# Half of the memory weight strips through one transfer and two engines, and the memory input prepared earlier

## The reference

```python
def first_block(x, mem, ...):
    hn = rmsnorm(h, norm_mix_g[l])
    proj = hn @ w_in[l]
    fq, fk, fv, ff, gq, gf, gi, gg = jnp.split(proj, split_idx, axis=-1)
    fox_out = fox_attention(to_heads(fq), to_heads(fk), to_heads(fv), log_f)   # 8 heads of 64
    rec = hgrn2_chunkwise(gq, gf, gi, lbs[l])                                  # 4 heads of 128
    rec = rmsnorm(rec, hgrn_norm_g[l]) * jax.nn.silu(gg)
    h = h + jnp.concatenate([fox_out, rec], axis=-1) @ w_out[l]
    mem_n = rmsnorm(mem, norm_mem_g[l])                                        # 256 x 1024
    h = h + memory_cross_attention(rmsnorm(h, norm_x_g[l]), mem_n, w_xq[l], w_xkv[l], w_xo[l])
    ...
# in memory_cross_attention: kv = mem_n @ w_kv (1024 x 2048), split into k and v
```

## Time and profile before

| | us |
|---|---|
| median of the three runs | 2054.51 |
| the three runs | 2054.51, 2051.1, 2054.57 |
| the profiled execution | 2046.84 |
| its span (first to last instruction) | 2044.7 |

### The profile page before, as it was taken

One profiled execution on the slowest core, in us unless ns is written; L12 is line 12 of the kernel. 1 busy time (PEld: TensorE's weight loads), 2 busy tenths in 40 slices (PEclk: granted clock), 3 DMA queues, 4 the chain that ended last, 5 costly groups with the idle time before them and its releaser, 6 DMA issues.

```text
span 2044.7 us, 26571 instructions
## 1 busy us (share of the span) xinstructions
PE 1924.6 (94%) x9426; PEld 1587.1 (78%) x9426; DVE 990.2 (48%) x1614; ACT 1101.0 (54%) x1526; POOL 272.1 (13%) x318
## 2 busy tenths in 40 slices
PE   5989978899899999999999999989999989999996
PEld 4777767787688888878878778878877868888885
DVE  4176643243442231446886777567661354223134
ACT  6545565452533333355478788668665454334342
POOL 1100001110111111111111111111111101111110
PEclk9999988899899999989999999999999999999998
DMA  8854548873789998978977667876869858898884
GB/s 240 177 114 104 124 112 195 176 166 83 164 192 194 192 193 192 195 158 186 198 155 175 153 145 170 214 183 145 225 144 216 189 121 198 191 196 192 193 179 105
DMA packets 96360, 349.94 MB, mean 171 GB/s; under 512 B 10712, under 2 KB 10712, under 8 KB 95744
## 3 DMA queue, kind: packets, MB, share of 16 engines
q0 software_dynamic: 45216, 163.60, 44.1%
q1 hardware_dynamic: 46512, 169.14, 29.9%
q10 hardware_dynamic: 4528, 15.81, 2.2%
HBM read 344.24 MB, written 4.28 MB: 170 GB/s over the span
## 4 chain that ended last, share of the span: by engine, by line
PE 73%; DVE 10%; ACT 6%; DMA 5%; issue 3%; DVEq 2%; ACTq 1%; SPq 0%
PE bank L350 19%; PE bank L352 19%; PE bank L351 19%; DVE ssum L1848 4%; DMA wl<-in_weights 3%; DMA arena<-scratch 2%; PE bank L459 2%; PE bank L460 1%; PE bank L461 1%; ACT wl L867 1%; PE work L428 1%; ACT wh L866 1%; DVE xt L1881 1%; PE bank L365 1%; PE bank L367 1%
## 5 line engine op out<-in xcount | busy, mean ns | idle before, releaser
L866 ACT ACTIVATE wh<-raw 128x1024 fp32r<-128x1024 f32 x314 | 331.9, 1057 | 649.6 <-PE bank L352 556.1
L350 PE MATMUL bank<-XAh,wh 128*128 128x512 f32 x1400 | 554.4, 396 | 24.5 <-DMA wl<-in_weights 22.6
L352 PE MATMUL bank<-XAh,wl 128*128 128x512 f32 x1400 | 547.1, 391 | 0.0
L351 PE MATMUL bank<-XAl,wh 128*128 128x512 f32 x1400 | 546.9, 391 | 0.0
L848 POOL DMA_DIRECT2D wl<-in_weights x314 | 271.9, 866 | 1739.6 <-ACT wl L867 1700.5
L350 PEld LDWEIGHTS bank<-XAh,wh 128*128 128x128 f32 x1400 | 264.4, 189 | 82.6 <-DMA wl<-in_weights 23.2
L867 ACT ACTIVATE wl<-raw 128x1024 fp32r<-128x1024 f32 x314 | 327.5, 1043 | 0.0
L352 PEld LDWEIGHTS bank<-XAh,wl 128*128 128x128 f32 x1400 | 264.0, 189 | 56.4
L351 PEld LDWEIGHTS bank<-XAl,wh 128*128 128x128 f32 x1400 | 264.7, 189 | 54.2 <-issue 0.7
L350 PE MATMUL bank<-XBh,wh 128*128 128x512 f32 x720 | 283.1, 393 | 9.6 <-DMA wl<-in_weights 9.6
L351 PE MATMUL bank<-XBl,wh 128*128 128x512 f32 x720 | 281.5, 391 | 0.0
(11 more groups left out here) (323 smaller groups left out, 2066.9 us busy)
## 6 DMA issues: line engine op xcount, KB each, us to landing
raw<-in_weights SPq DMA_DIRECT2D x306, 512.0 KB, 7.3
wl<-in_weights POOLq DMA_DIRECT2D x306, 512.0 KB, 8.0
arena<-scratch ACTq DMA_DIRECT2D x20, 512.0 KB, 7.9
raw<-in_weights SPq DMA_DIRECT2D x8, 384.0 KB, 4.5
wl<-in_weights POOLq DMA_DIRECT2D x8, 384.0 KB, 6.0
h<-in_xT SPq DMA_DIRECT2D x2, 1024.0 KB, 6.5
spill<-cst ACTq DMA_DIRECT2D x8, 256.0 KB, 6.0
arena<-spill ACTq DMA_DIRECT2D x1, 2048.0 KB, 10.8
```

The lines of the kernel that those rows point to most:

```text
L350: mm(bank[s][:, 0:w], hi, tile(X[0], k, w), start=(n == 0), stop=False)
L351: mm(bank[s][:, 0:w], hi, tile(X[1], k, w), start=False, stop=False)
L352: last = mm(bank[s][:, 0:w], lo, tile(X[0], k, w), start=False, stop=(n == len(kts) - 1))
L866: act_(wh[j % 4][:, :], raw[j % 2][:, :], ACT.Copy)
```

## The change

Of the 16 memory strips every other one (29, 31, ... 43: `DIRECT`) no longer goes through `raw`. SP loads it once into `wraw`, which is the memory of `wl` seen as plain float, when strip j - 4 is done; ACT rounds it to `wh` (`round_direct`) and DVE writes `wraw - wh` over it (`sub_direct`), for which PE waits (`w_sub`). POOL issues no second transfer for it. The tables `staged_before`, `lows` and `direct_turn` count the strips on each way. In the memory stage ACT makes its `step`s ahead of `fox_first` in steps with s % 3 == 0, always ahead of `fox_stored` and of the four SiLUs of step 1, and one `mem_turned` ahead of the last two `step`s. The memory's input is loaded at s = 0 of head 3; its squares are made on ACT at s = 4 to 7 into free space and summed on DVE at l = 6, 7 (six) and at the end (two), apart from the high and low parts, which come at s = 8, 9 on ACT and in turns of 2, 4 and 2 on DVE, with no signal from DVE. PE takes 14 memory triples into steps 9, 10, 11 of head 3 (2, 4, 8) and 9 or 10 into each step of the memory stage.

```diff
-MEM_FILLS = [10, 11, 11] * 4
+MEM_LEAD = {9: 2, 10: 4, 11: 8}
+MEM_FILLS = [9, 10] * 6
+DIRECT = [AT["mem"] + m for m in range(0, 2 * KT, 2)]
...
+        wraw = [sb(f"wraw{s}", [P, STRIP]) for s in range(4)]      (same place as wl)
+        mem_sq = [hkk[:, n * NMEM:(n + 1) * NMEM] for n in range(6)] + [hqq[...] for n in (4, 5)]
...
+            def low_ready(j, i=None, per=4):
+                if j in DIRECT:
+                    pe.wait_ge(w_sub, DIRECT.index(j) + 1)
+                else:
+                    pe.wait_ge(w_lo[j % 4], val(16 * lows(j), i, 4 * per))
...
                     fill("fox", n - min(n, 1))
+                    if t == HG - 1:
+                        fill("mem", MEM_LEAD.get(s, 0), tiles_from("mem"), NMEM)
...
+            def load(j):
+                a = staged_before(j)
+                sp.wait_ge(w_neg, a - 1)
+                sp.dma_start(raw[a % 2][:, 0:w.shape[1]], w).then_inc(raw_ready[a % 2], 16)
+            def load_direct(j):
+                sp.wait_ge(strip_done, j - 3)
+                sp.dma_start(wraw[j % 4][:, :], weights[j]).then_inc(w_in[j % 4], 16)
+            first = AT["xq"] + 1
+            n = 2
+            for d in DIRECT:
+                while n <= min(d + 3, AT["w_out"]):
+                    if n not in DIRECT:
+                        load(n)
+                    n += 1
+                load_direct(d)
...
+            ROUND_AT = {(AT["mem"] - 1 if d == AT["mem"] + 2 else d - 2): d for d in DIRECT}
+            def round_direct(j):
+                act.wait_ge(w_in[j % 4], 16 * direct_turn(j))
+                act_(wh[j % 4][:, :], wraw[j % 4][:, :], ACT.Copy).then_inc(w_rounded, 1)
             def step(j, i=None, per=4, last=False):
-                if j + 4 < NS and not last:
+                if j + 4 < NS and not last and j + 4 not in DIRECT:
                     act.wait_ge(strip_done, val(j + 1, i, per))
                     high(j + 4, i, per)
+                if j in ROUND_AT:
+                    round_direct(ROUND_AT[j])
...
             for s in range(STEPS):
-                fox_first(HG - 1, s)
+                if s % 3:
+                    fox_first(HG - 1, s)
+                for m in MEM_DONE[s - 1]:
+                    step(AT["mem"] + m)
+                if s % 3 == 0:
+                    fox_first(HG - 1, s)
...
                 fox_stored(HG - 1, s)
                 if s == 1:
                     ...the four SiLUs
-                for m in MEM_DONE[s - 1]:
-                    step(AT["mem"] + m)
...
             fox_store(HG - 1, TT - 1)
+            for m in MEM_DONE[STEPS - 2]:
+                mem_turned(m - KT)
             for m in MEM_DONE[STEPS - 1]:
                 step(AT["mem"] + m)
-            for m in MEM_DONE[STEPS - 2] + MEM_DONE[STEPS - 1]:
+            for m in MEM_DONE[STEPS - 1]:
                 mem_turned(m - KT)
...
+            def sub_direct(j):
+                if j in DIRECT:
+                    dve.wait_ge(w_rounded, DIRECT.index(j) + 1)
+                    TTop(wl[j % 4][:, :], wraw[j % 4][:, :], wh[j % 4][:, :].bitcast(F32), ALU.subtract).then_inc(w_sub, 1)
...                                           (HGRN, t == HG - 1:)
+                    if t == HG - 1 and l > 5:
+                        for n in range(3 * l - 18, 3 * l - 15):
+                            mem_sum(n)
                 gather(t, LEVELS - 1)
+                if t == HG - 1:
+                    sub_direct(AT["mem"])
...
-            low_tile(mem_in[KT - 1], V("mem_g", KT - 1), KT - 1, "mem", NMEM)
+            sub_direct(AT["mem"] + 2)
+            for n in range(6, KT):
+                mem_sum(n)
...                                           (end of mem_in_strip:)
+                if n > 0:
+                    sub_direct(j + 2)
```

More of the change, by code:

```diff
@@ L163, with staged_before, lows, direct_turn @@
 FOX_DONE = strips_done([n for f in FILLS for n in f], LEAD)
-MEM_DONE = strips_done(MEM_FILLS)
+MEM_DONE = strips_done(MEM_FILLS, sum(MEM_LEAD.values()))
+DIRECT = [AT["mem"] + m for m in range(0, 2 * KT, 2)]
+def staged_before(j):
+    return j - sum(d < j for d in DIRECT)
+def lows(j):
+    return sum(n % 4 == j % 4 for n in range(j + 1) if n not in DIRECT)
+def direct_turn(j):
+    return sum(d % 4 == j % 4 for d in DIRECT if d <= j)
 def block_kernel(nc, xT, memT, weights, weights6, vectors, consts, scratch, spill, outT):
@@ L185, in block_kernel @@
         wh = [sb(f"wh{s}", [P, STRIP], F32R) for s in range(4)]
-        wl = [sb(f"wl{s}", [P, STRIP], F32R) for s in range(4)]
+        with ExitStack() as low_views:
+            wl = [low_views.enter_context(nc.sbuf_tensor(f"wl{s}", [P, STRIP], F32R)) for s in range(4)]
+        wraw = [sb(f"wraw{s}", [P, STRIP]) for s in range(4)]
         vec = sb("vec", [P, NVEC])
@@ L306, in block_kernel @@
         for name, tiles, sqs, norms in [
[L307 removed]
+            ("in", KT, KT, 1), ("mem", KT, 0, 1), ("rec", 4, 0, 0), ("fox", 4, 0, 0), ("w_out", KT, KT, 1),
             ("xattn", KT, 0, 0), ("xo", KT, KT, 1), ("hid", 4 * KT, 0, 0), ("final", 0, KT, 1),
@@ L846, in low @@
                 w = weights[j] if j < NS_FULL else weights6[j - NS_FULL]
-                pool.wait_ge(w_neg, j + 1)
+                pool.wait_ge(w_neg, staged_before(j) + 1)
                 pool.dma_start(wl[j % 4][:, 0:w.shape[1]], w, accum_op=ALU.add).then_inc(w_lo[j % 4], 16)
-            def lows(j, end):
-                for n in range(j, end):
-                    low(n)
-            lows(0, NS)
+            for j in range(NS):
+                if j not in DIRECT:
+                    low(j)
         @block.scalar
@@ L1650, in _ @@
                 if t == HG - 1:
-                    for n in range(3):
+                    for n in range(2):
                         mem_low(n)
@@ L1664, in _ @@
                 if t == HG - 1:
-                    for n in range(3, 6):
+                    for n in range(2, 6):
                         mem_low(n)
```

68 lines of the change are left out of this document (41 added, 27 removed).

## The result

Five runs of the changed kernel gave a median of 2024.64 us (2022.84 to 2028.26) against 2054.51 (2051.1 to 2062.25): **29.9 us faster**, ratio 0.986, 95% interval 0.9839 to 0.9882. The forecast was 19.7 us and the range ended at 27.7, so the time lies outside it. The pair of profiled executions differs by less: 2026.92 against 2046.84, 19.9 us. The same two kernels measured again, twice, gave 0.987 (0.984 to 0.9899) and 0.9902 (0.987 to 0.9933), 27.1 and 23.1 us by medians, both inside the range of gains, 9.5 to 27.7. The mean of the three gains is 26.7 us (25.1 if each is worked out from its ratio); I explain that, and come back to why the first number is at its upper end.

What follows compares the result with a forecast made beforehand. TensorE was taken to be held in the memory stage by strips' second transfers and ScalarE's order. Gains of 3.0 up to strip 4, 15.3 to w_out and 1.4 of clock make 19.7 us: 2054.5 - 19.7 = 2034.8 us, range 2027 to 2045.

Steps and rivals of the forecast that it cites:

- Tail of the last head: End of the last HGRN head: PE waits some 3.5 us ahead of the turn at 266; norm starts at about 287.
- Strip 4: First direct strip PE reaches in the memory stage: subtracted at 300.9, PE waits over 4 us, 3.0 us gained up to here.
- X: From strip 4 to w_out: allowance for what is late next, taken as 5 us, between none and about 12.
- 49.9: From strip 4 to w_out: 34.6 us of triples at full clock plus 15.3 of attention, spreads and turns.
- three near misses: Memory stage: subtractions of strips 8, 10 and 14 come within 0.5 us of PE, none behind it.
- rival 2: Memory stage: no wait left, X = 0 and strip 4 waits under 2 us; gain 24.7 + 3, 2027 us; chance 0.10.
- The base: From strip 4 to w_out the kernel before takes 376.8 - 303.9 = 72.9 us, from which the gain is counted.
- The DMA share: Memory stage: share stays close to 0.85, so landing times stay, 9.1 us for POOL's transfers and 4.9 for SP's.
- Start of `w_out`: End of memory stage: the 4.42 us wait goes, with 1.4 us of low clock; w_out begins at about 357, not 376.8.
- Rival 4: Memory stage: ACT's and PE's order alone set it, not the transfers; gain about 5 us or less, 2051 us; chance 0.06.
- The rule on DVE and POOL: Direct subtractions beside POOL's transfer issues: no cost counted; by the skill's rule eight would add 10 us of delay at most.
- The chances: Whole kernel: forecast 0.60, rivals 0.18, 0.10, 0.06 and 0.06; faster 0.89, within 0.2% 0.04, slower 0.07.

Runs made afterwards that it cites:

- order_only: Kernel before with only ScalarE's new memory-stage order (strips' steps ahead of attention copies, stores and SiLUs; one mem_turned earlier) and a fox_refill earlier in step 1: ratio 0.9964.
- old_order: Changed kernel with ScalarE's memory-stage order as before, direct strips and early triples kept: ratio 0.9946.
- no_direct: Changed kernel with no direct strip, all 16 memory strips staged, the new ScalarE order and early triples kept: ratio 0.9882.
- tail_mended: Changed kernel with the SiLUs one step later, and DVE's sums of squares 3 to 5 and first direct subtraction moved later in the last head: ratio 0.9862.
- after_again: Changed kernel measured a second time without any edit, against the kernel before: ratio 0.987.
- after_third: Changed kernel measured a third time without any edit, against the kernel before: ratio 0.9902.

## Why the prediction was right and wrong, point by point

- **Tail of the last head.** Right in place and size: the wait ahead of the turn, expected at 3.5 us, was 3.36 in all three profiles; the norm started at 286.1 (expected 287).
- **Strip 4.** Right: 299.40 (expected 300.9), releaser DVE, 3.8 us, because of ACT's list. 4.5 us earlier than before in the first pair instead of 3.0, of which 1.0 is the start-up; from the 151st matmul it is 4.0 by the means.
- **X, what is late next. This is the term that failed.** I took 5 us of new waits and 2.7 of low clock on 49.9. The walk through the steps had found no wait; I added 5 us because three subtractions came within 0.5 us of need. The measured stretch is 351.60 - 299.40 = 52.2 us: 2.3 over 49.9, for X and clock together, instead of 7.7, and the same within 0.02 us in all three profiles. The clock behind the wait at strip 4 is part of it:
```profile
299.40:304.00 4.60, 4.60 (x26) 4.60 (x27) 0.84 (x4) 1.64 (x2) 0.86 (x1) 0.63 0.59 144
```
A clock of 0.63 over 4.6 us is about 3.4 us at the low level where I took about 6, and by the two paces of a triple that costs 1.5 us, not 2.7. So X is about 0.8 us instead of 5. PE's only waits over 0.5 us behind strip 4 are two of 0.57 and 0.59 us for ACT, at 349.38 and 351.43. The three near misses, the subtractions of strips 8, 10 and 14, didn't turn into waits in any of three executions. In this stretch rival 2 is what happened; its other half, a short wait at strip 4, is not.
- **The base.** The 72.9 us of before in this stretch, from which the sum starts, are the longest of three (66.1 and 70.2). That pulls the other way: from the mean, 69.7, the same sum would have given 3.2 us less.
- **The DMA share.** I held it at 0.85 and so kept the old landing times. 0.85 was that of one stretch, 336.4 to 360; the whole stage had 0.72, and the 77 us of transfers in a stage of 90 that seemed to agree with it did so by chance. It fell to 0.68. POOL's transfers in the stage landed a little earlier by the median, the direct ones later than the 4.9 us I took, and PE waited for a direct strip only at strip 4 (280 to 352 us; for `wraw` all eight):
```profile
DMA to landing us min/median/max: 7.6/8.3/9.5
...
DMA to landing us min/median/max: 4.4/7.1/8.7
```
- **Start of `w_out`.** 4.42 us gone, as named. From the first matmul of `w_out` to the 1001st after it the three profiles of before take 242.7 to 243.0 us and those of the changed kernel 240.1 to 241.0, 1.7 to 2.9 less, where I had 1.4 for the low clock; order_only takes 239.8, old_order 243.3, so it comes with the order. My sign for the start of `w_out`, 357, already had that 1.4 in it; the sum gives 358.5.
- **Which cause.** The prediction listed the transfers first and ACT's order second. The runs turn this round: the order is worth 6 us of mark alone (order_only), 8 with the early triples and the preparation, and 19 with the direct strips as well (old_order); the direct strips 3.6 with it and nothing without it. Rival 4, that the transfers weren't it, had the causes more nearly right than the forecast and the size wrong, about 5 us against the 22.5 that no_direct gained. The sum didn't suffer, as it was made from waits and not from causes.
- **The rule on DVE and POOL.** POOL's issues kept their length (ns min/median/max), so no cost, as counted. But the run hardly tests it: of the eight issues one lies over a subtraction of two SBUF inputs, by 0.18 us. The Trainium skill (SBUF — State Buffer, Who interferes with whom) says that such a DVE instruction contends with a GpSimd instruction that reads SBUF and not with one that only writes it. That the issue at 339.52 took 0.86 us like the others doesn't speak against the second case, and isn't enough to show it:
```profile
L899 POOL DMA_DIRECT2D wl<-in_weights x8: 862/862/867, 291.7 to 346.0; - x8
...
339.52 0.86 POOL L899 DMA_DIRECT2D wl<-in_weights  x1 [4.18 <-ACT wl L917]
...
340.21 1.23 DVE L1444 TENSOR_TENSOR wl<-wraw,wh 128x1024 fp32r<-128x1024 f32 x1 [2.56 <-ACT wh L922]
```
- **From one profile to the median.** I carried the profiled difference over to the medians and gave the range no term for scatter. The two profiles differed by 19.9 us and the medians by 29.9. That 19.9 is so near the 19.7 of the forecast is luck: at the start of `w_out` the profiles were already 25.2 us apart, and then the changed one took 7.9 us longer in the stretch near 1480 us (93.2 there, 85.3 in that of before), a spot that scatters with nothing changed. Whether the timed runs differ by that spot isn't shown. And before scatters by 6.7 us in this stage and by 14.5 in the rest; its medians beside the five groups of runs were 2054.5, 2048.5, 2046.5, 2045.4 and 2045.2, the first, on which the forecast stands, the highest. Of the 10.2 us between forecast and first result, 5.4 are X and the clock behind strip 4, about 1 the start of `w_out` and about 1 strip 4; the rest, some 3 us, lies within this scatter, and the third measurement, 23.1 us, needs none of it. By my estimate the range should have reached lower by 3 to 5 us for that alone.
- **The chances.** 0.60, 0.18, 0.10 and half of rival 4's 0.06 make 0.91 for faster, not 0.89.

## What to carry to other kernels

When a strip pipeline stalls at a transfer, look at what the engine ahead of that transfer does before it: here ScalarE stood at attention results while strips it could have rounded were waiting, and in a new order, with some work moved ahead, the same transfers fitted at a DMA share of 0.88 and gave most of the gain. A new order moves the waits to whatever now stands behind a late transfer, and a cheaper way in for some of the strips then takes those away; under the old order it gave nothing. Such a way has a price of its own, here 4.8 us ahead of strip 4 for 8.3 behind it, and two moves in the orders of ACT and DVE (tail_mended) took that price away. Where a walk through the steps finds no wait, don't add one for comfort: put the doubt in the range, with the kernel's own scatter, which two executions of the kernel before would have shown.

## What was unexpected in the hardware

- The same program differed by up to 6.7 us in one stage of 90 and 14.5 us in the 1650 behind it from execution to execution, on a core by itself; with the waits for transfers gone from the stage, that part went too (three executions of the changed kernel: 0.5 us in the mark, 0.02 from strip 4 on).
- Waits of 2.2 to 5 us of TensorE were mostly followed by several us at its lower level: six matmuls of 128 columns took 1.54 us after 3.36 us of wait in the changed kernel, and 0.88 after 0.97. In after_again and after_third they took 0.88 after the same 3.36 us, so the length of the wait alone doesn't decide it:
```profile
267.56 0.88 PE L457 MATMUL work<-cst,arena 128*128 128x128 f32 x6 [3.36 <-DVEq L1672]
```
